# Down projection of three row blocks as seven block products, with the block sums made on GpSimd

## The chip, the cores and the metric

One core of one Trainium2 chip runs the whole program. The metric is the device time of one execution in microseconds (us), as the median of several runs. The engines are called PE (matrix products), DVE (vector), ACT (activations), POOL (GpSimd) and SP (which issues transfers).

## What is computed

The reference is one step of a one-layer trunk: an mLSTM and a gated MLP side by side, an output projection, and then a SwiGLU channel mixer. It runs over 2048 prompt rows and 8 sample rows, all in float32. The part that is changed is the last product, `@ w_down`:

```
h2 = rmsnorm(x, g_norm2) * (1 + sc2) + sh2
a, bb = jnp.split(h2 @ w_gate_up, 2, axis=-1)     # (T, 1024) @ (1024, 5632)
x = x + gt2 * ((jax.nn.silu(a) * bb) @ w_down)    # (T, 2816) @ (2816, 1024)
...
y = rmsnorm(x, g_final)
```

## The kernel before

The 2048 prompt rows go through in four blocks of 512 rows (`BLK`, `NBLK`). Every block passes the same stages: 24 slabs of `w_in` with the mixers in between, 8 slabs of `w_out`, the norm, 44 slabs of `w_gate_up`, and 22 slabs of `w_down`. Block 0 also carries the preparation of the modulation. The last block also carries the samples, and its down projection is not touched by the change.

Each float32 operand is split into a high part of reduced precision (`fp32r`) and the rest: `hi = round(x)`, `lo = x - hi`. A product is then three matmuls, hi by lo, lo by hi and hi by hi. A weight slab of 128x1024 elements lands in one of two slots of `raw` (a transfer that SP issues), ACT writes `w_hi` from it (`split_hi`), DVE writes `w_lo = raw - w_hi` (`split_lo`), and PE then uses both. The split of a slab may begin when PE is through with the slab two places earlier, and `raw` is loaded again when the slot's low part is done.

In the down stage a slab holds two k-tiles of 128 rows and half of the 1024 columns. PE runs over the block's four row tiles with it (`tile_product`), so a slab is 4 x 2 x 3 = 24 matmuls of 128x128 by 128x512. The first eleven slabs make the left 512 columns, the other eleven the right. After each half DVE takes the four PSUM banks, multiplies by the gate `gt2` and adds to `x1` (`down_tiles`). The activations, `act_hi` and `act_lo`, come from the gate-up stage, where `gate_tile` on DVE multiplies the two halves, ACT makes the high part and DVE the low part.

Beside this, the down stage prepares the next block: POOL loads the next 512 rows into `x_sb` and computes a root (`root`), ACT squares and scales, DVE scales (`scale_left`), PE transposes eight tiles (`norm_out`), ACT and DVE write `hT_hi` and `hT_lo` from them (`next_tiles`, `norm_tiles`). The order on each engine is written out by hand; engines wait for each other by semaphores, and every queue is worked off in order.

Of the kernel before, what the change touches and what calls it, by code (L numbers as in the profile page):

```python
# [29 lines left out]
P = 128  # L30
# [33 lines left out]
NSLAB = S_DOWN + N_DOWN  # L64
NORM_AT = (5, 7)
# [42 lines left out]
def hybrid_step(nc, x_prompt, x_sample, c_prompt, c_sample, state_C, state_n, state_m, w_ada, b_ada,  # L108
# [4 lines left out]
    with ctx:  # L113
# [29 lines left out]
        w_lo, WL = new("w_lo", [P, 2, KT, P], F32R)  # L143

# [15 lines left out]
        hm = place("hm", [P, TT, H, P], F32, U + 16 * kb)  # L160

# [116 lines left out]
        proj_rows = nc.dram_tensor("proj_rows", [NB, N_IN], F32).ap()  # L278

# [20 lines left out]
        DOWN_BANK = [T[0], T[1], G[0], G[1]]  # L300

# [20 lines left out]
        tile_ps = signal("tile_ps", 4 * (TT - 1))  # L322
        out_read = signal("out_read", 4 * TT, 1)
# [61 lines left out]

        def each_head(ap, n=P):

            return ap.unsqueeze(2).broadcast_to([ap.shape[0], ap.shape[1], n])
# [38 lines left out]
        def _(sp):  # L427
# [12 lines left out]
            def load_in(blk, s):  # L440
                c = IN_COLS[s % NSLAB]
                load(blk, s, in_v[:, :, c:c + P], KT)

# [12 lines left out]
            def sample_loads(s):  # L456
# [12 lines left out]
                if s == 6:  # L469
                    sp.wait_ge(sem("vo_ps"), 1)  # L470
# [27 lines left out]
            def sp_block(blk):  # L498
# [15 lines left out]
                for n in range(N_DOWN):  # L514
                    j, q = divmod(n, DOWN_Q)
                    load_pair(blk, S_DOWN + n, down_v, q, j)
                    if n == DOWN_Q + 4:
                        sp.wait_ge(out_read.sem, out_read.at(blk, 3 * TT))
                        gate_row(gt2_in, work[:, 1], 1, BLK, D)
                for s in (NSLAB, NSLAB + 1):  # L520
                    load_in(blk, s)
# [45 lines left out]
        def _(pool):  # L567
# [67 lines left out]
            def samples_state():  # L635
                pool.wait_ge(sem("wexp"), 2)
# [5 lines left out]
            def samples_mixing():  # L642
                done = sem("hcm")
                pool.wait_ge(sem("vars"), 1)
# [15 lines left out]
            def pool_block(blk, last):  # L660
# [4 lines left out]
                for c in range(TT):  # L665
# [11 lines left out]
                    if last and c == 0:  # L677
                        pool.wait_ge(sem("msml"), 1)
# [17 lines left out]
                if not last:  # L696
                    pool.wait_ge(zadd.sem, zadd.at(blk, 2 * TT))
# [36 lines left out]
            with pool.Fori(0, NBLK - 1) as blk:  # L734
                pool_block(blk, False)
# [4 lines left out]
        def _(act):  # L740
# [62 lines left out]
            def for_samples(step):  # L803

                if step == "SG":
                    act.wait_ge(sem("proj_in"), 48)
                    act.activation(proj[:, GATE0:], proj[:, GATE0:], ACT.Gelu_apprx_tanh)\
                        .then_inc(sem("gelus"), 1)
                    act.wait_ge(sem("nAs"), 1)
                    act.activation(sm["e"][:, :], sm["nA"][:, :], ACT.Exp).then_inc(sem("logs"), 1)  # L810
                    act.wait_ge(sem("logs"), 1)
                    act.activation(sm["l"][:, :], sm["e"][:, :], ACT.Ln, bias=1.0).then_inc(sem("logs"), 1)
                elif step == "SW":
                    act.wait_ge(sem("wargs"), 1)
                    act.activation(sm["quant"][:, 4:12], sm["quant"][:, 4:12], ACT.Exp)\
                        .then_inc(sem("wexp"), 1)
                    act.activation(sm["em"][:, :], sm["m"][:, :], ACT.Exp, scale=-1.0)\
                        .then_inc(sem("wexp"), 1)
                    fetch("small_out", m_sample[0], sm["m"][:, :])
                elif step == "SC":  # L820
                    act.wait_ge(sem("oTs"), 1)
                    act.activation(colq[:, 10], colq[:, 1], ACT.Sigmoid).then_inc(sem("sigs"), 1)
# [27 lines left out]
            def scale_right(blk):  # L850

                act.wait_ge(rs.sem, rs.at(blk, MEANS[1]))
                for i in range(TT):
# [4 lines left out]
            def norm_tile(blk, n, k, a_col, b_col):  # L858
# [4 lines left out]
                act.activation(work[:, 2 + k % 2], ps[:, :], ACT.Identity,  # L863
# [48 lines left out]
            def act_block(blk, last, first=False):  # L912
# [54 lines left out]
                def gate_pairs(pair_i):  # L967
                    for u in range(2):
# [3 lines left out]
                        if last and u == 1:  # L972
# [4 lines left out]
                        act.activation(act_hi[:, bass.ds(pair_i * 2 + u, 1), :], work[:, 3:4, :], ACT.Copy)\  # L977
                            .then_inc(act_hi_done.sem, 1)
# [25 lines left out]
                for n in range(N_DOWN):  # L1004
# [1258 lines left out]
```

## Time and profile before

| what | us |
|---|---|
| median of three runs (2477.85 to 2480.75) | 2479.61 |
| span of the profiled execution, first to last instruction | 2477.8 |
| PE busy in it | 2427.0 |
| DVE, ACT, POOL busy in it | 1203.8, 846.1, 176.9 |
| down stage of block 1, from 1121.56 to 1244.83 | 123.27 |
| of this DVE busy, ACT busy, POOL busy | 46.06, 36.48, 1.03 |

The page gives the profiled execution by its span alone; no time around it is listed for it. The median of the runs is 1.8 us above that span, the lowest run equal to it to 0.1 us. A matmul's row shows 0.39 us, but matmuls overlap in the pipeline: their cost is the distance from one start to the next. "Idle before" in a group is the time in which the engine stood still just ahead of that instruction, with what ended it.

### The profile page before, as it was taken

How to read it: one execution, taken by the hardware profiler on the slowest of the kernel's cores; microseconds unless marked ns; L12 is line 12 of the kernel's file. 1: busy time of each engine (PE TensorE's matmuls, PEld its weight loads, DVE VectorE, ACT ScalarE, POOL GpSimd, SP SyncE). 2: the span in 40 equal slices, each digit the busy share in tenths (PEclk: the TensorE clock that was granted, in tenths of full speed). 3: DMA queues.
4: the chain of work that ended last, by engine and by line, in shares of the span. 5: the costliest groups of instructions: out<-in, count | busy, mean ns of one | idle time of the engine just before them, and what ended most of it. 6: DMA issues, size and time to landing. Idle time of an engine off the chain costs nothing.

```text
span 2477.8 us, 32788 instructions
## 1 busy us (share of the span) xinstructions
PE 2427.0 (98%) x12296; PEld 1979.9 (80%) x12296; DVE 1203.8 (49%) x1773; ACT 846.1 (34%) x1152; POOL 176.9 (7%) x143
## 2 busy tenths in 40 slices
PE   5999999999999999999999999999999999999998
PEld 4688877888888878888888878888888878888776
DVE  4648544434346554444354754443449754333323
ACT  2333422233244243334143343333236323333212
POOL 0022000000003000000002200000002400000001
PEclk8999999999999999999999999999999999999999
DMA  7822365332352333332342233333255322222222
GB/s 280 287 80 90 111 196 164 118 95 96 91 147 66 101 111 99 96 93 94 103 140 78 90 111 98 97 93 102 94 185 160 92 77 69 85 85 85 89 90 86
DMA packets 361045, 280.14 MB, mean 113 GB/s; under 512 B 11289, under 2 KB 302653, under 8 KB 360920
## 3 DMA queue, kind: packets, MB, share of 16 engines
q1 hardware_dynamic: 333012, 228.91, 30.5%
q10 hardware_dynamic: 23956, 34.81, 4.1%
q0 software_dynamic: 3968, 14.95, 1.6%
q8 instruction: 71, 1.16, 0.2%
q14 instruction: 38, 0.30, 0.0%
HBM read 267.68 MB, written 10.96 MB: 112 GB/s over the span
## 4 chain that ended last, share of the span: by engine, by line
PE 89%; DVE 5%; issue 2%; DMA 2%; ACT 1%; POOL 0%; DVEq 0%; SPq 0%; ACTq 0%; POOLq 0%
PE banks L1862 18%; PE banks L1863 18%; PE banks L1864 18%; PE banks L1915 9%; PE banks L1916 8%; PE banks L1917 8%; PE banks L1742 1%; DVE w_lo L1337 1%; DMA stage<-in_w_ada_dram 1%; PE banks L1876 1%; PE banks L2004 1%; PE banks L2061 1%; PE banks L1886 1%; PE banks L1938 1%; PE banks L2030 1%
## 5 line engine op out<-in xcount | busy, mean ns | idle before, releaser
L1862 PE MATMUL banks<-hT_hi,w_lo 128*128 128x512 f32 x2176 | 859.9, 395 | 3.1 <-DVE hT_lo L1343 1.6
L1864 PE MATMUL banks<-hT_hi,w_hi 128*128 128x512 f32 x2176 | 848.6, 390 | 0.0
L1863 PE MATMUL banks<-hT_lo,w_hi 128*128 128x512 f32 x2176 | 848.5, 390 | 0.0
L1337 DVE TENSOR_TENSOR w_lo<-raw,w_hi 128x1024 fp32r<-128x1024 f32 x392 | 493.3, 1258 | 579.5 <-ACT w_hi L848 567.7
L848 ACT ACTIVATE w_hi<-raw 128x1024 fp32r<-128x1024 f32 x392 | 412.7, 1053 | 465.7 <-PE banks L1917 437.4
L1862 PEld LDWEIGHTS banks<-hT_hi,w_lo 128*128 128x128 f32 x2176 | 409.3, 188 | 100.6 <-issue 9.3
L1864 PEld LDWEIGHTS banks<-hT_hi,w_hi 128*128 128x128 f32 x2176 | 409.0, 188 | 86.2
L1863 PEld LDWEIGHTS banks<-hT_lo,w_hi 128*128 128x128 f32 x2176 | 409.4, 188 | 81.3
L1915 PE MATMUL banks<-w_lo,act_hi 128*128 128x512 f32 x704 | 276.2, 392 | 0.0
L1916 PE MATMUL banks<-w_hi,act_lo 128*128 128x512 f32 x704 | 274.2, 390 | 0.0
L1917 PE MATMUL banks<-w_hi,act_hi 128*128 128x512 f32 x704 | 274.1, 389 | 0.0
L1675 DVE TENSOR_TENSOR work<-work,banks 128x512 f32<-128x512 f32 x88 | 60.5, 688 | 271.9 <-ACT work L971 271.9
L977 ACT ACTIVATE act_hi<-work 128x512 f32 (+1 forms) x88 | 55.6, 632 | 371.8 <-DVE work L1679 371.8
L1915 PEld LDWEIGHTS banks<-w_lo,act_hi 128*128 128x128 f32 x704 | 132.1, 188 | 32.0 <-issue 4.5
L1917 PEld LDWEIGHTS banks<-w_hi,act_hi 128*128 128x128 f32 x704 | 132.1, 188 | 27.8
L1916 PEld LDWEIGHTS banks<-w_hi,act_lo 128*128 128x128 f32 x704 | 132.2, 188 | 26.7
L1679 DVE TENSOR_TENSOR work<-work,banks 128x512 f32<-128x512 f32 x88 | 60.6, 689 | 190.1 <-PE banks L1864 190.1
L587 POOL TENSOR_TENSOR rrt<-msq,half 128x1 f32<-128x1 f32 (+1 forms) x27 | 18.2, 676 | 1424.2 <-DVE msq L1098 1168.2
L971 ACT ACTIVATE work<-banks 128x512 f32<-128x512 f32 x88 | 52.6, 598 | 187.3 <-PE banks L1864 186.9
L1915 PE MATMUL banks<-w_lo,mix_hi 128*128 128x512 f32 x256 | 100.4, 392 | 1.8 <-DVE w_lo L1337 1.1
L1916 PE MATMUL banks<-w_hi,mix_lo 128*128 128x512 f32 x256 | 99.8, 390 | 0.0
L1917 PE MATMUL banks<-w_hi,mix_hi 128*128 128x512 f32 x256 | 99.6, 389 | 0.0
(335 smaller groups left out, 1828.9 us busy)
## 6 DMA issues: line engine op xcount, KB each, us to landing
raw<-in_w_gate_up_dram SPq DMA_DIRECT2D x176, 512.0 KB, 3.6
raw<-in_w_in_dram SPq DMA_DIRECT2D x96, 512.0 KB, 3.7
raw<-in_w_down_dram SPq DMA_DIRECT2D x88, 512.0 KB, 3.6
ada_stage<-in_w_ada_dram ACTq DMA_DIRECT2D x8, 2048.0 KB
raw<-in_w_out_dram SPq DMA_DIRECT2D x32, 512.0 KB, 3.6
in_stage<-in_w_in_dram ACTq DMA_DIRECT2D x6, 2048.0 KB
stage<-in_w_ada_dram SPq DMA_DIRECT2D x4, 2048.0 KB
x_sb<-in_x_prompt_dram POOLq DMA_DIRECT2D x4, 2048.0 KB, 8.8
```

The costliest lines, as they stand in the source:

```text
L848: act.activation(w_hi[:, s % 2], raw[:, s % 2], ACT.Copy).then_inc(hi_done.sem, 1)
L971: act.activation(work[:, 2], G[0][:, :], ACT.Sigmoid).then_inc(evac.sem, 1)
L977: act.activation(act_hi[:, bass.ds(pair_i * 2 + u, 1), :], work[:, 3:4, :], ACT.Copy)\
L1337: ve.tensor_tensor(w_lo[:, s % 2], raw[:, s % 2], w_hi[:, s % 2].bitcast(F32), ALU.subtract).then_inc(lo_done.sem, 1)
L1675: ve.tensor_tensor(work[:, 2], work[:, 2], G[0][:, :], ALU.mult).then_inc(silu_done.sem, 1)
L1679: ve.tensor_tensor(work[:, 3], work[:, 2], G[1][:, :], ALU.mult).then_inc(gated.sem, 1)
L1862: mm(out, w_lo[:, slot, k, :], rhs_hi[:, r, :], start=start and n == 0, stop=False)
L1863: mm(out, w_hi[:, slot, k, :], rhs_lo[:, r, :], start=False, stop=False)
L1864: ins = mm(out, w_hi[:, slot, k, :], rhs_hi[:, r, :], start=False, stop=stop and last)
L1915: mm(out, x_hi[:, k0 + k, t], lo[:, k, :], start=start and k == 0, stop=False)
L1916: mm(out, x_lo[:, k0 + k, t], hi[:, k, :], start=False, stop=False)
L1917: ins = mm(out, x_hi[:, k0 + k, t], hi[:, k, :], start=False, stop=stop and k == 1)
```

## The change

In blocks 0 to 2 the product A @ B of the down stage is cut in two by two: A by row halves (256 rows each) and by even and odd k-tiles, B by even and odd k-tiles and by column halves. Instead of the eight block products there are seven (the form of Strassen's scheme with 15 sums), named in the order in which they run: P1, P2, P5, P6, P7, P3, P4. Each has 11 k-tiles, two row tiles and 512 columns, so 66 matmuls of the same shape as before.

- **Weights.** The four sums of blocks of B are computed once, in block 0, by POOL (`down_sums`): 11 rounds of a 1 MB load, four subtractions of 128x512 and a 1 MB store to `wd_scratch` in DRAM. SP waits for all of them (`wd_out`) before it loads the first slab of P5 in each block. A product has six slabs of 2, 2, 2, 2, 1 and 2 k-tiles, 42 per block where there were 22, and they rotate through three slots: the two old ones and a third (`raw2` with `w2` or `w3`). The split of a slab may begin when PE is through with the slab three places earlier.
- **Activations.** `gate_tile` writes the float32 products into `quad`. High and low parts are made there for the row half that P1 and P2 use. POOL makes the four sums of blocks of A (`quad_sums`, `total`), each in pieces of 4, 4 and 3 k-tiles by 256 columns. For P5, P6, P7, P3 and P4 ACT makes the high parts (`high_part`) and POOL the low parts (`low_parts`), in the same pieces.
- **Results.** ACT copies P1 out of PSUM while P2 goes on accumulating on it. DVE joins the other products (`rows_11`, `sums_u`, `rows_with`), between its splits.
- **Next block.** The load of `x_sb` stands behind the sums on POOL, and its steps (squares, root, scaling, transposes) move to later slabs.
- **Names.** A number of one-time semaphores are merged (`STEPS`, `once`); that changes no instruction's work.

```diff
+SEVEN_K = ((0, 2), (2, 4), (4, 6), (6, 8), (8, 9), (9, QM))
+NSEV = 7 * len(SEVEN_K)
+PIECES = ((0, 4), (4, 8), (8, QM))
+P1, P2, P5, P6, P7, P3, P4 = range(7)
+NORM_AFTER = {31: (0, 1), 33: (2, 3), 37: (4, 5), 39: (6, 7)}
+SQUARES_AT = (20, 21, 22, 23)
+MEAN_AT, LEFT_AT, RIGHT_AT = 25, 28, (28, 29)
...
+            def down_sums():
+                pool.wait_ge(zadd.sem, zadd.at(0, 2 * TT))
...
+                for m in range(QM):
...
+                    pool.dma_start(wd_in[:, :, :], pairs_v[m]).then_inc(sem("wd_in"), 16)
+                    pool.wait_ge(sem("wd_in"), 16 * (m + 1))
...
+                    pool.tensor_tensor(wd_sums[:, 0], b12, b11, ALU.subtract).then_inc(done, 1)
...
+                    pool.dma_start(wd_scratch[:, :, m, :].rearrange("q p n -> p q n"), wd_sums[:, :, :])\
...
+            def quad_sums(blk):
+                def total(first, out, a, b, op):
+                    for i, (m0, m1) in enumerate(PIECES):
+                        pool.tensor_tensor(out(m0, m1), a(m0, m1), b(m0, m1), op).then_inc(quad_sum.sem, 1)
...
+                def low_parts(prod):
+                    for i, (m0, m1) in enumerate(PIECES):
+                        pool.wait_ge(part_hi.sem, part_hi.at(blk, n))
...
+                        pool.tensor_tensor(lo, piece_source(prod, m0, m1), hi.bitcast(F32), ALU.subtract)\
+                            .then_inc(part_lo.sem, 1)
+                pool.wait_ge(gated.sem, gated.at(blk, FT))
+                pool.wait_ge(act_ready.sem, act_ready.at(blk, FT))
+                total(0, s, a21, a22, ALU.add)
+                total(3, a21, a11, a21, ALU.subtract)
+                low_parts(P5)
+                total(6, s, s, a11, ALU.subtract)
+                low_parts(P6)
+                total(9, a12, a12, s, ALU.subtract)
...
                 if not last:
-                    pool.wait_ge(zadd.sem, zadd.at(blk, 2 * TT))
+                    if first:
+                        down_sums()
+                    low_parts = quad_sums(blk)
                     pool.dma_start(x_sb[:, :, :], x_v[bass.ds(blk + 1, 1)].rearrange("o p i d -> p (o i) d"))\
                         .then_inc(x_in.sem, 16)
                     pool.wait_ge(x_in.sem, x_in.at(blk, 32))
                     pool.sem_inc(x_next.sem, 1)
+                    low_parts(P7)
+                    low_parts(P3)
                     root(blk, 1)
+                    low_parts(P4)
...
+            def split_hi_seven(blk, n):
...
+                act.wait_ge(done.sem, done.at(blk, count))
+                act.wait_ge(slab_used.sem, slab_used.at(blk, S_DOWN + max(n - 2, 0)))
...
+                act.activation(sev_flat(dst, m1 - m0), sev_flat(src, m1 - m0), ACT.Copy).then_inc(hi_done.sem, 1)
...
+            def split_lo_seven(blk, n):
...
+                ve.wait_ge(hi_done.sem, hi_done.at(blk, S_DOWN + n + 1))
...
+                ve.tensor_tensor(lo, src, hi.bitcast(F32), ALU.subtract).then_inc(lo_done.sem, 1)
...
+            def gained(blk, i, row, j, gate, src):
+                link(ve.tensor_tensor(both(work[:, 0]), src, gate, ALU.mult))
+                out = x1[:, row, j * BLK:(j + 1) * BLK]
+                ve.tensor_tensor(out, out, work[:, 0], ALU.add).then_inc(zadd.sem, 1)
...
+            def rows_with(blk, prod, j, gate, parts, row0, count):
+                for i in range(2):
+                    product_ready(blk, prod, i)
+                    link(ve.tensor_tensor(both(work[:, 0]), parts[i], both(SEVEN_BANK[prod][i]), ALU.add))
...
+                    gained(blk, 2 * TT + count + i + 1, row0 + i, j, gate, both(work[:, 0]))
...
-                for n in range(1, N_DOWN + 1):
-                    if n < N_DOWN or not last:
-                        split_lo(blk, S_DOWN + n)
...
+                split_lo(blk, S_DOWN + 1)
+                for n in range(NSEV + 1):
+                    seven_out(blk, n)
+                    if n + 2 < NSEV:
+                        split_lo_seven(blk, n + 2)
...
+            def seven_products(blk):
+                for n in range(NSEV):
...
+                    pe.wait_ge(lo_done.sem, lo_done.at(blk, S_DOWN + n + 1))
+                    for i in range(2):
...
+                        for m in range(m0, m1):
...
+                            if i == 0 and prod > P2 and m % 4 == 0:
+                                pe.wait_ge(part_lo.sem, part_lo.at(blk, 3 * (prod - P5) + m // 4 + 1))
...
+                            mm(out, x_hi, low, start=start, stop=False, skip_group_check=True)
+                            mm(out, x_lo, high, start=False, stop=False, skip_group_check=True)
+                            ins = mm(out, x_hi, high, start=False, stop=stop, skip_group_check=True)
...
+                    ins.then_inc(slab_used.sem, 1)
+                    if n in NORM_AFTER:
...
+                        norm_out(blk, NORM_AFTER[n])
```

On POOL, in the loop over blocks, these rows stood between the last root of the norm (`rrt<-msq,half 128x1`) and the root for the next block (`128x4`); ISA and REGISTER_ALU rows are waits:

```order
L587 TENSOR_TENSOR rrt<-msq,half 128x1
L697 ISA
L698 ISA
L698 DMA x_sb<-in_x_prompt_dram 128x4x1024
L700 REGISTER_ALU
L595 REGISTER_ALU
L587 TENSOR_TENSOR rrt<-msq,half 128x4
```

At the same place POOL now begins with these; `s_quad` and `quad` are sums of activation blocks, `part` the high and low parts, and a size of 128x4x256 is 1024 elements per partition:

```order
L808 ISA
L809 REGISTER_ALU
L793 TENSOR_TENSOR s_quad<-quad 128x1024 x2
L793 TENSOR_TENSOR s_quad<-quad 128x768
L794 ISA
L793 TENSOR_TENSOR quad<-quad 128x4x256 x2
L793 TENSOR_TENSOR quad<-quad 128x3x256
L794 REGISTER_ALU
L802 ISA
L804 TENSOR_TENSOR part<-s_quad,part 128x4x256
```

Until the row that loads `x_sb` there are 18 of these operations in all, and 9 more follow it; before there was none.

On DVE, at the end of the left half of the down stage, the four tiles of results followed on a split (two of the four are shown; `x_56` is `x1`):

```order
L1337 TENSOR_TENSOR w_lo<-raw,w_hi 128x1024
L1506 ISA
L1482 REGISTER_ALU
L1514 TENSOR_TENSOR work<-banks,work 128x512
L1074 REGISTER_ALU
L1516 TENSOR_TENSOR x_56<-x_56,work 128x512
```

Now DVE comes to its first results, those of P2, after the split of slab 13, and the next row is the split of slab 14:

```order
L1747 TENSOR_TENSOR w_lo<-raw,w_hi 128x1024
L1766 ISA
L1752 ISA
L1769 TENSOR_TENSOR work<-banks,work 128x512
L1286 REGISTER_ALU
L1772 TENSOR_TENSOR x_56<-x_56,work 128x512
L1769 TENSOR_TENSOR work<-banks,work 128x512
L1286 REGISTER_ALU
L1772 TENSOR_TENSOR x_56<-x_56,work 128x512
L1745 REGISTER_ALU
L1747 TENSOR_TENSOR w_lo<-raw_61,w_hi 128x1024
```

So each group of results stands in front of the split of the slab that PE uses two slabs later.

## Rows read from the trace of the kernel before

**Rows 1.** Page, head and part 1: busy time, share of span, instructions of each engine.
```profile
span 2477.8 us, 32788 instructions
PE 2427.0 (98%) x12296; PEld 1979.9 (80%) x12296; DVE 1203.8 (49%) x1773; ACT 846.1 (34%) x1152; POOL 176.9 (7%) x143
```

**Rows 2.** Windows, gate-up stage of block 0 and down stage of block 1; columns in line 1.
```profile
core 0: us, PE busy (x) PEld busy (x) DVE busy (x) ACT busy (x) POOL busy (x), PEclk, DMA share, GB/s
284.00:542.00 258.00, 257.68 (x1214) 204.49 (x1213) 124.18 (x154) 75.58 (x96) 0.85 (x1) 1.00 0.47 148
1121.70:1244.70 123.00, 123.00 (x561) 102.23 (x560) 46.06 (x57) 36.48 (x43) 1.03 (x1) 1.00 0.30 97
```

**Rows 3.** Timeline of PE, down stage of block 1, first matmuls and last: start us, us, what.
```profile
1121.56 0.39 PE L1915 MATMUL banks<-w_lo,act_hi 128*128 128x512 f32 x1
1121.78 0.39 PE L1916 MATMUL banks<-w_hi,act_lo 128*128 128x512 f32 x1
...
1244.60 0.39 PE L1917 MATMUL banks<-w_hi,act_hi 128*128 128x512 f32 x1
1244.83 0.39 PE L1984 MATMUL banks<-hT_lo,gw 128*128 128x512 f32 x1
```

**Rows 4.** Chain of waits, one of block 1's two rows of transposes: start, us, what.
```profile
1154.37 1.75 PE banks L1961 x16
```

**Rows 5.** Groups by line and form: count, busy us, mean ns, idle before.
```profile
L848 ACT ACTIVATE w_hi<-raw 128x1024 fp32r<-128x1024 f32 x392 | 412.7, 1053 | 465.7 <-PE banks L1917 437.4 <-DMA raw<-in_w_in_dram 16.8 <-DMA raw<-in_w_down_dram 9.1
L1337 DVE TENSOR_TENSOR w_lo<-raw,w_hi 128x1024 fp32r<-128x1024 f32 x392 | 493.3, 1258 | 579.5 <-ACT w_hi L848 567.7 <-issue 0.9 <-DVE proj_gates L1156 0.3
L1516 DVE TENSOR_TENSOR x<-x,work 128x512 f32<-128x512 f32 x32 | 22.2, 693 | 4.8 <-DVE work L1514 3.5
L1342 DVE CAST hT_hi<-work 128x512 fp32r<-128x512 f32 x64 | 27.0, 422 | 28.6 <-ACT work L863 28.3
L706 POOL TENSOR_TENSOR x<-x,g_fin 128x512 f32<-128x512 f32 x4 | 5.0, 1283 | 122.6 <-ACT junk L766 122.6
L689 POOL TENSOR_TENSOR vs_tm<-vs_tm,rln 128x2048 f32<-128x2048 f32 x4 | 14.4, 3612 | 0.7 <-DVE vs_tm L1449 0.7
```

**Rows 6.** Timelines of POOL and DVE in block 0: two collisions, one operation alone.
```profile
206.21 3.61 POOL L689 TENSOR_TENSOR vs_tm<-vs_tm,rln 128x2048 f32<-128x2048 f32 x1 [0.16 <-DVE vs_tm L1449]
206.74 4.17 DVE L1337 TENSOR_TENSOR w_lo<-raw,w_hi 128x1024 fp32r<-128x1024 f32 x1 [0.64 <-ACT w_hi L848]
...
177.70 2.09 POOL L629 TENSOR_TENSOR hm<-hm,rml 128x512 f32<-128x512 f32 x1
177.66 1.22 DVE L1337 TENSOR_TENSOR w_lo<-raw,w_hi 128x1024 fp32r<-128x1024 f32 x1 [1.14 <-ACT w_hi L848]
...
218.73 1.04 POOL L629 TENSOR_TENSOR hm<-hm,rml 128x512 f32<-128x512 f32 x1
```

**Rows 7.** Timelines of POOL and DVE in block 0: overlap without a delay.
```profile
157.36 1.29 POOL L621 TENSOR_TENSOR decay<-decay,mask 128x512 f32<-128x512 f32 x1
157.14 0.69 DVE L1420 TENSOR_TENSOR work<-banks,col 128x516 f32<-128x516 f32 x1
```

**Rows 8.** Timeline of PE behind the first collision of rows 6.
```profile
212.81 0.39 PE L1864 MATMUL banks<-hT_hi,w_hi 128*128 128x512 f32 x1
213.77 0.46 PE L2061 MATMUL banks<-wT,vs_tm 128*128 128x128 f32 x2 [0.57 <-DVEq L1422]
```

**Rows 9.** Windows at the program's start; PEclk is the third column from the end.
```profile
28.00:34.00 6.00, 0.90 (x7) 0.00 (x0) 3.56 (x7) 1.06 (x1) 1.04 (x1) 0.50 1.02 347
34.00:38.00 4.00, 3.90 (x20) 3.62 (x24) 1.51 (x4) 0.00 (x0) 0.64 (x1) 0.50 0.56 153
38.00:40.00 2.00, 2.00 (x18) 0.44 (x11) 0.09 (x1) 0.00 (x0) 0.00 (x0) 0.97 0.39 115
```

**Rows 10.** Page, part 6, DMA issues: KB each, us from issue to landing.
```profile
raw<-in_w_down_dram SPq DMA_DIRECT2D x88, 512.0 KB, 3.6
x_sb<-in_x_prompt_dram POOLq DMA_DIRECT2D x4, 2048.0 KB, 8.8
```

More of the change, by code:

```diff
@@ L661, in pool_block @@
+            def pool_block(blk, last, first=False):
                 if last:
@@ L732, in sample_root @@
                 power(sem("s_root"), s_r[:, :], s_ms[:, :], NB, P)
-            with pool.Fori(0, NBLK - 1) as blk:
+            pool_block(0, False, first=True)
+            with pool.Fori(1, NBLK - 1) as blk:
                 pool_block(blk, False)
@@ new lines, in sums_u @@
+            def sums_u(blk):
+                for i in range(2):
+                    product_ready(blk, P6, i)
+                    ve.wait_ge(u_set.sem, u_set.at(blk, i + 1))
+                    ve.tensor_tensor(work[:, 2 + i], work[:, 2 + i], SEVEN_BANK[P6][i], ALU.add).then_inc(sev_read.sem, 1)
+                for i in range(2):
+                    ve.wait_ge(sev_read.sem, sev_read.at(blk, 3 + i))
+                    ve.tensor_tensor(t_sum[i], both(work[:, 2 + i]), both(SEVEN_BANK[P5][i]), ALU.add)\
+                        .then_inc(sev_read.sem, 1)
@@ L1690, in ve_block @@
                     thin_in_rows(TH_IN + N_TH_IN - 1)
-                with ve.Fori(2 * N_TH_IN if first else 0, FT) as i:
-                    gate_tile(i)
+                if last:
+                    with ve.Fori(0, FT) as i:
+                        gate_tile(i)
+                else:
+                    with ve.Fori(N_TH_IN if first else 0, QM) as m:
+                        for kappa in range(2):
+                            gate_tile(m * 2 + kappa, m, kappa)
                 ve.wait_ge(slab_used.sem, slab_used.at(blk, S_DOWN))
@@ L2189, in pe_block @@
                     pe.transpose(N2[0:H, 0:P], CN[:, :, P], ident[:, :]).then_inc(sem("fin_ps"), 1)
-                for n in range(N_DOWN):
+                if not last:
+                    seven_products(blk)
+                for n in range(N_DOWN if last else 0):
                     j, q = divmod(n, DOWN_Q)
@@ L2221, in pe_block @@
                         samples()
-                    if n in NORM_AT and not last:
-                        c = 4 * NORM_AT.index(n)
-                        norm_out(blk, range(c, c + 4))
             pe_block(0, False, first=True)
```

372 lines of the change are left out of this document (288 added, 84 removed).

## The prediction

> **What bounds the kernel now.** I read the page's busy shares first: PE is busy for 2427.0 of 2477.8 us, no other engine for half of that [rows 1]. [...] The stage runs from 1121.56 to 1244.83, that is 123.27 us [rows 3]. Two transpose rows of 1.75 us lie in it [rows 4], so its 528 matmuls take 119.77 us and one costs 0.2268 us. That is the price of a matmul here; the 0.39 us in its row is the length in the pipeline. So fewer matmuls pay in full, as long as the other engines keep the splits ahead. In this stage a split by ACT takes 1.05 us and one by DVE 1.22 [rows 5, 6], and a slab gives PE 24 x 0.2268 = 5.44 us of work.
>
> **The change part by part.**
>
> Matmuls. Seven products of 66 are 462 instead of 528 per block. 66 x 0.2268 = 14.97 us go per block, and PE's own work in the stage becomes 123.27 - 14.97 = 108.3 us. Over three blocks that is 44.9 us, 1.8%. The transposes stay.
>
> Slabs. Each is now half as long for PE, 12 x 0.2268 = 2.72 us (the sixth one-k-tile slab of a product, 1.36), while its split costs the same, for ACT 1.05 and for DVE 1.22. By the third slot a split may start two slabs, 5.44 us, before PE needs it. 1.05 + 1.22 = 2.3 us fit, with 3.1 to spare. At the start there is less: slab 1 waits for the last gate-up slab, then a DVE product (0.69, as the row of L1516 [rows 5]), a high part of 256 columns (between a quarter and a half of the 1.05 us for 1024, say 0.4) and both splits, 3.4 us against 2.72, so 0.7 us are lost. The loads land 3.6 us after issue [rows 10] and start when the slab three places earlier is split, so I cost them at nothing; their cover is those same 5.44 us and more.
>
> POOL's sums. Per block 27 operations, 18 of 1024 elements per partition and 9 of 768. POOL needs 1.283 us for 512 elements from two different operands [rows 5]. With one operand broadcast it needs 1.04 for 512 and 3.612 for 2048 [rows 5, 6], so 1.674 ns per element and 0.18 us fixed. With that fixed part the first price gives 2.15 ns per element: 2.39 us for 1024, 1.83 for 768, in all 9 x (2 x 2.39 + 1.83) = 59.5 us. The lower bound is the broadcast rate, 1.90 and 1.47, in all 47.4 us; 1.283 us for each 512, with nothing saved by length, would be 63.5 us at the top. I take 59.5, since L706 reads two full operands as these sums do. [...]
>
> What these sums do to DVE. The trace shows that POOL and DVE do not work side by side when both read two operands from SBUF. At 206.21 POOL began an operation of 3.61 us; DVE's split issued at 206.74 ended at 210.91, after 4.17 us instead of 1.22 [rows 6]. The other way round, at 177.66 a split of 1.22 us was running, and POOL's 1.04 us became 2.09 [rows 6]. A DVE operation with one operand in PSUM was not held up: 0.69 us under POOL's 1.29 [rows 7]. So I count the time of such operations on both engines as one resource. Whole operations alternate, not their elements.
>
> The sum of that resource, from the end of gate-up until P4 begins (36 slabs; the low parts for P4 are due there too). POOL: 59.5. DVE: 31 full splits at 1.22 are 37.8, six half ones at 0.69 are 4.2, six operations on results with both operands in SBUF at 0.69 are 4.2, a low part 0.35, four scalings at 0.42 and four tiles of the next block at 0.42 + 0.69 are 6.1; in all 52.6 (the 0.69 and 0.42 from L1516 and L1342 [rows 5]). Together 112.1 us. PE has 396 x 0.2268 + 1.75 = 91.6 us of work in the same stretch. So the bound moves from PE to what POOL and DVE share, by 20.5 us. P4 with its transposes adds 66 x 0.2268 + 1.75 = 16.7 us, undisturbed: 128.8. The shared resource also stands idle once: POOL waits 8.8 us for the load of `x_sb` [rows 10], while DVE can split only as fast as PE frees slots, 8.8 / 2.72 x 1.22 = 3.9 us. That leaves 4.9 us idle, and the low parts for P7 and P3 queue behind the wait. The stage becomes 133.7 us, 10.4 longer than before: 15.0 us of matmuls saved, 25.4 us of waits gained.
>
> Where they fall: at slabs 1 and 2, where POOL's six sums start as gate-up ends; at each short slab of P1 and P5, where 1.36 us of matmuls cover a pair of 2.39 + 1.22; and, largest, some 6 us each at slabs 14 and 32, where DVE has two to four result operations in front of the split and POOL gets a turn before each.
>
> The weights' sums. 44 operations of 128x512 in block 0, 44 x 1.28 = 56 us, in a stage of 258 us where DVE is busy for 124 [rows 2]. A split there has 3.1 us to spare and meets one operation of 1.28, seldom two. I take 1 us; bounds 0 and 5 (0.5 us for ten slabs). Their transfers, 22 of 1 MB, go beside slabs that land with 7 us to spare.
>
> Block ends. The results of P4 reach `x1` some 4 us after the last matmul, under the 16 gate matmuls (3.6 us) with which PE begins the next block; I cost that at nothing, 0.5 us a block if the cover fails.
>
> Sum: 3 x 10.4 + 1 = 32 us. The profiled span is 2477.8 and the median 2479.6; I add to the median: 2511.6, rounded to 2511.
>
> **The rivals.**
>
> A, faster: the collisions are absorbed. After the 4.17 us split PE had matmuls until 212.81 and stood still for only 0.57 us, on another wait [rows 8]. If POOL and DVE meet as rarely as that, the stage takes 108.3 plus the 0.7 at its start and up to 3.5 us behind the result groups, 109 to 112.5 us, and the time is 2480 - 3 x 11 to 14, some 2444. It decides from the point where collisions cost PE less than 15.0 of the 25.4 us per block counted above. Against it: there the slab was 5.44 us long and the collision single.
>
> B, no change: POOL works at the broadcast rate. 47.4 in place of 59.5 leaves 3 x 1.7 us less than before by the sum, or a little over it where turns do not mesh: 2474 to 2486, say 2480. For it, that L706 is only 512 elements long; against, that the operand that repeats is what makes the other rows cheap.
>
> C, slower still. Waits of 6 us can bring the clock down. [...] Two such waits per block are 12 us in all. And 2 MB for `x_sb` now land beside twice the weight traffic; 3 us later is 9 us over three blocks. Together 2532. [...]
>
> D, the weight sums are not there in time for P5 of block 0. They have 258 us for 11 rounds, 23 us each; a round is 5.1 us of sums, and two transfers of 1 MB, by half of 8.8 each, 14 us in all. I give it no chance of its own.
>
> **How the numbers follow.** The forecast, 2490 to 2525, has 0.53; C 0.12; B 0.14; A 0.21. Faster than 0.2% (below 2474.6, about what a measurement of this kernel can tell) is A: 0.21. Within 0.2% is most of B: 0.10. Slower is the rest: 0.69. The range reaches into A and takes in B and most of C, 2466 to 2536.
>
> **What would show it.** In the profile of the changed kernel: matmul distance still 0.227 us; down stages of 130 to 137 us in blocks 0 to 2 with some 25 us of PE idle, ended by `w_lo`, most at slabs 1, 5, 14, 17 and 32; POOL's pieces at 2.4 us or more each; the mean of the DVE split in these stages near 2.5 us in place of 1.26; PE without waits in the last block. Right in mechanism but wrong in size would be splits that are held up while PE idles under 10 us per stage. Wrong altogether would be splits near 1.3 us beside POOL's sums.

## The result, and the profile after

The changed kernel takes 2532.41 us (median of 4 runs, 2531.02 to 2533.86), the kernel before beside it 2479.34 (2477.85 to 2480.75): a ratio of 1.0215, 95% interval 1.0201 to 1.0230. It is 53 us slower; the prediction said 32 slower, with 2466 to 2536 as its range.

The page of the changed kernel, head and part 1, answers to [rows 1]:

```profile
span 2532.2 us, 33213 instructions
PE 2414.6 (95%) x12098; PEld 1955.0 (77%) x12098; DVE 1398.1 (55%) x1863; ACT 925.6 (37%) x1263; POOL 487.1 (19%) x290
```

PE has 198 matmuls fewer, as was meant (3 x 66). Yet it is busy for only 12.4 us less, and the span grew by 54.4. DVE is busy for 194 us more and POOL for 310.

The down stage of block 1 in windows that are cut at PE's three long waits; it answers to the second row of [rows 2], and the columns are the same:

```profile
1147.50:1151.00 3.50, 0.46 (x3) 0.05 (x1) 3.33 (x2) 2.03 (x3) 3.50 (x2) 1.00 0.00 0
1151.00:1157.00 6.00, 6.00 (x19) 4.75 (x20) 6.00 (x3) 0.63 (x1) 5.92 (x3) 0.72 0.43 121
...
1187.50:1193.20 5.70, 0.36 (x2) 0.00 (x0) 5.42 (x4) 1.36 (x2) 5.70 (x3) 0.94 0.00 0
1193.20:1199.20 6.00, 5.97 (x14) 4.72 (x15) 5.42 (x2) 0.45 (x1) 5.92 (x3) 0.50 0.65 192
...
1245.50:1252.20 6.70, 0.33 (x3) 0.09 (x2) 6.54 (x4) 2.55 (x4) 5.50 (x3) 0.87 0.00 0
1252.20:1258.20 6.00, 5.99 (x16) 4.76 (x17) 3.67 (x6) 0.58 (x1) 0.00 (x0) 0.57 0.74 248
```

In the windows of 3.5, 5.7 and 6.7 us PE does next to nothing, while DVE is busy nearly all the time and POOL for most of it. In the 6 us behind each PE is busy throughout, at a granted clock of 0.72, 0.50 and 0.57 (at 0.50 a matmul starts every 0.43 us, in place of every 0.227). That costs (1 - clock) x 6 us: 1.7 + 3.0 + 2.6 = 7.3 us.

PE's timeline: the stage's first matmul, the ends of these waits, and the row behind the stage; it answers to [rows 3]:

```profile
1145.03 0.39 PE L2245 MATMUL banks<-w_lo,part 128*128 128x512 f32 x1
...
1150.95 0.49 PE L2245 MATMUL banks<-w_lo,part 128*128 128x512 f32 x1 [3.04 <-DVE w_lo L1549]
...
1193.23 0.79 PE L2245 MATMUL banks<-w_lo,part 128*128 128x512 f32 x1 [5.37 <-DVE w_lo L1747]
...
1252.21 0.79 PE L2245 MATMUL banks<-w_lo,part 128*128 128x512 f32 x1 [6.38 <-DVE w_lo L1747]
...
1282.80 0.39 PE L2320 MATMUL banks<-hT_lo,gw 128*128 128x512 f32 x1
```

All three are waits for a slab's low part from DVE, at slabs 1, 14 and 32. The last row is the first matmul of the next block, so the stage ends at 1282.80, after 137.77 us; those of blocks 0 and 2 took 134.69 and 137.07.

DVE's groups by form in this stage (count, busy us, mean ns, idle before), which answer to the splits in [rows 5]:

```profile
L1747 DVE TENSOR_TENSOR w_lo<-raw,w_hi 128x1024 fp32r<-128x1024 f32 x33 | 65.0, 1994 | 19.3 <-ACT w_hi L1022 18.5 <-DVE x L1760 0.5
L1747 DVE TENSOR_TENSOR w_lo<-raw,w_hi 128x512 fp32r<-128x512 f32 x7 | 11.3, 1608 | 2.6 <-ACT w_hi L1022 2.6
```

What stood at 1.22 and 0.69 us takes 1.99 and 1.61 here. The instructions are the same; the rest is waiting that the profile counts as their own time. POOL's row for the stage shows the other side, 77.96 us busy where the sum had 59.5 plus a root.

So the 54.4 us of the span are: the down stages +11.4, +14.5 and +13.8 us (39.7 together), the gate-up stage of block 0 +11.9 (the first down stage starts at 554.21, before it was 542.27), 0.9 between the down stages, and some 2 us behind the last one.

### The profile page after: what moved, and what is told of

Read it like the earlier page. It is cut to its first block, busy times and chain, and to the rows that moved or that the text cites. A ratio compares the mean times of both kernels' runs of the same rounds, so it can differ in the third digit from the quotient of the medians.

```text
span 2532.2 us, 33213 instructions
## 1 busy us (share of the span) xinstructions
PE 2414.6 (95%) x12098; PEld 1955.0 (77%) x12098; DVE 1398.1 (55%) x1863; ACT 925.6 (37%) x1263; POOL 487.1 (19%) x290
## 3 DMA queue, kind: packets, MB, share of 16 engines
q8 instruction: 70, 1.15, 0.2%
## 4 chain that ended last, share of the span: by engine, by line
PE 72%; DVE 11%; DMA 5%; POOL 5%; issue 4%; ACT 2%; DVEq 0%; SPq 0%; ACTq 0%; POOLq 0%
PE banks L2165 17%; PE banks L2166 17%; PE banks L2167 17%; PE banks L2218 4%; PE banks L2219 4%; PE banks L2220 4%; DVE w_lo L1747 3%; DMA raw<-in_w_gate_up_dram 2%; DVE w_lo L1549 2%; POOL s_quad L793 1%; POOL quad L793 1%; POOL part L804 1%; PE banks L2045 1%; PE banks L2245 1%; DMA stage<-in_w_ada_dram 1%
## 5 line engine op out<-in xcount | busy, mean ns | idle before, releaser
L1549 DVE TENSOR_TENSOR w_lo<-raw,w_hi 128x1024 fp32r<-128x1024 f32 x332 | 430.1, 1296 | 416.5 <-ACT w_hi L1012 407.1
L1012 ACT ACTIVATE w_hi<-raw 128x1024 fp32r<-128x1024 f32 x326 | 342.8, 1051 | 250.5 <-PE banks L2220 208.4
L1747 DVE TENSOR_TENSOR w_lo<-raw,w_hi 128x1024 fp32r<-128x1024 f32 (+1 forms) x120 | 228.1, 1931 | 62.0 <-ACT w_hi L1022 60.1
L2245 PE MATMUL banks<-w_lo,part 128*128 128x512 f32 x462 | 192.8, 417 | 55.6 <-DVE w_lo L1747 46.2
L1957 DVE TENSOR_TENSOR work<-work,banks 128x512 f32<-128x512 f32 x88 | 60.5, 688 | 272.0 <-ACT work L1171 272.0
L2246 PE MATMUL banks<-w_hi,part 128*128 128x512 f32 x462 | 187.1, 405 | 0.0
L2247 PE MATMUL banks<-w_hi,part 128*128 128x512 f32 x462 | 186.7, 404 | 0.0
L1022 ACT ACTIVATE w_hi<-raw 128x1024 fp32r<-128x1024 f32 (+1 forms) x120 | 117.6, 983 | 186.9 <-PE banks L2247 122.6
L2245 PEld LDWEIGHTS banks<-w_lo,part 128*128 128x128 f32 x462 | 91.4, 198 | 88.5 <-issue 40.9
L793 POOL TENSOR_TENSOR s_quad<-quad 128x1024 f32<-128x1024 f32 (+1 forms) x9 | 25.4, 2843 | 588.9 <-DVE part L1965 588.9
L1963 DVE TENSOR_TENSOR quad<-work,banks 128x512 f32 (+1 forms) x66 | 45.4, 688 | 152.7 <-PE banks L2167 152.7
L2247 PEld LDWEIGHTS banks<-w_hi,part 128*128 128x128 f32 x462 | 90.9, 197 | 20.5
L2246 PEld LDWEIGHTS banks<-w_hi,part 128*128 128x128 f32 x462 | 91.5, 198 | 18.1
```

Source lines behind the costliest of these rows:

```text
L1012: act.activation(w_hi[:, s % 2], raw[:, s % 2], ACT.Copy).then_inc(hi_done.sem, 1)
L1022: act.activation(sev_flat(dst, m1 - m0), sev_flat(src, m1 - m0), ACT.Copy).then_inc(hi_done.sem, 1)
L1549: ve.tensor_tensor(w_lo[:, s % 2], raw[:, s % 2], w_hi[:, s % 2].bitcast(F32), ALU.subtract).then_inc(lo_done.sem, 1)
L1747: ve.tensor_tensor(lo, src, hi.bitcast(F32), ALU.subtract).then_inc(lo_done.sem, 1)
L2245: mm(out, x_hi, low, start=start, stop=False, skip_group_check=True)
L2246: mm(out, x_lo, high, start=False, stop=False, skip_group_check=True)
```

## The experiments

Two places were to be explained: the down stages, and block 0's gate-up stage. The table has all runs. "Start" is the first matmul of block 0's down stage; stages are from there to the next block's first gate matmul; "between" runs from the end of one down stage to the start of the next, over blocks 1 and 2. All in us. Stages are read from the profiled execution, the time is the median; E8's profiled execution took 2449.9, 4 less than its median. E1, E2, E3, E6, E7 and E9 are one run each, E4, E5 and E8 eight, eleven and five.

| kernel | start | down stages | between | time |
|---|---|---|---|---|
| before | 542.3 | 123.3, 123.3, 123.3 | 456.0, 456.1 | 2479 |
| changed | 554.2 | 134.7, 137.8, 137.1 | 456.1, 456.9 | 2532 |
| E1 small sums | 548.6 | 111.8, 113.7, 112.3 | 456.1, 456.9 | 2454 |
| E2 powers of 4 columns | 558.7 | 113.2, 114.3, 114.1 | 456.1, 456.9 | 2471 |
| E9 powers of 10 columns | 554.4 | 115.1, 115.2, 114.2 | 456.1, 457.1 | 2469 |
| E3 low parts on DVE | 551.2 | 128.7, 128.9, 129.3 | 456.1, 457.2 | 2506 |
| E7 split first | 548.7 | 133.4, 137.0, 136.7 | 456.2, 456.7 | 2524 |
| E6 first round later | 546.5 | 135.2, 138.4, 136.6 | 456.1, 457.8 | 2528 |
| E4 early, paced | 549.2 | 119.6, 121.2, 121.1 | 458.9, 459.7 | 2485 |
| E5 spread | 549.4 | 117.0, 116.0, 116.6 | 461.9, 463.2 | 2477 |
| E8 aligned | 543.1 | 112.3, 113.4, 112.6 | 456.1, 457.4 | 2454 |

### Is it what POOL does, or the new order of the slabs?

E1 cuts POOL's 27 sums per block to 8 columns (where so cut, P5 and P6 take their activations from `quad`):

```diff
-pool.tensor_tensor(out(m0, m1), a(m0, m1), b(m0, m1), op).then_inc(quad_sum.sem, 1)
+pool.tensor_tensor(out(m0, m1)[:, :, 0:8], a(m0, m1)[:, :, 0:8], b(m0, m1)[:, :, 0:8], op)...
```

> Left out: in the down stages of blocks 0 to 2 POOL's 27 sums are made for 8 of 256 columns only, so what P5, P6, P7, P3 and P4 multiply is not the reference's; the weights' sums in block 0 stay whole. Theory (POOL's and DVE's operations on two SBUF operands take turns): with POOL's operations this short, the turns are gone. The down stages of blocks 1 and 2, 137.8 and 137.1 us, become 109 to 114 (108.3 of PE's own work and 1 to 6 of starts and result groups), PE's gaps of 3.0, 5.3 and 5.8 us at slabs 1, 14 and 32 shrink below 1.5, and the granted clock in them is 1.00 again. Gate-up of block 0 stays 12 us longer than before. Time 2532 - 23 - 2 x 25 = 2459, between 2450 and 2468. Rival 1 (the half-length slabs and their order are at fault, not the sums): stages stay above 130, time above 2510. Rival 2 (the clock falls for another reason than the waits): gaps go, but the mean clock of the stages stays at 0.95.

Measured: 2454.0 us. In block 1 the gap at slab 1 is 1.15 us, at slab 14 there is none, at slab 32 it is 0.6; the largest of all is 1.4, at slab 20. The stage as one window, in columns as in [rows 2], and DVE's full splits in it:

```profile
1116.45:1230.10 113.65, 109.47 (x496) 89.75 (x494) 71.39 (x86) 68.23 (x81) 12.85 (x29) 1.00 0.62 194
...
L1748 DVE TENSOR_TENSOR w_lo<-raw,w_hi 128x1024 fp32r<-128x1024 f32 x33 | 40.2, 1227 | 34.1 <-ACT w_hi L1023 33.1 <-DVE x L1761 0.5
```

The mean granted clock is 1.00 over the stage, and the splits take 1.23 us again. The 42 short slabs and the longer chain of results cost 3.5 to 5.4 us beside PE's 108.3, no more (111.8 to 113.7). Rivals 1 and 2 fall, and the matmuls saved do pay in full.

E2 and E9 keep POOL at work but let it touch little. A power of a few columns is slow on POOL for its size, 1.14 to 1.17 us for the 4 columns of E2 and 2.01 to 2.10 for the 10 of E9 (E9's edit):

```diff
-pool.tensor_tensor(lo, piece_source(prod, m0, m1), hi.bitcast(F32), ALU.subtract)
+pool.tensor_tensor(lo[:, 0, 0:10], onerow[:, 0:10], half[:, 0:10], ALU.pow)
```

> Left out: POOL's 27 sums per block are replaced by a power of 4 columns of constants, some 2.5 us each, so POOL is about as long at work but touches little; and in block 0, 40 of the 44 subtractions of weights are made for 8 columns only, while their transfers stay whole. Theory (turns): in the trace of before a POOL power of 3.8 us did not hold a DVE split up, so the down stages become 109 to 118 us although POOL is as busy as in the changed kernel, and DVE's splits return to 1.2 to 1.4 us. Rival (POOL is simply late with sums and low parts): stages stay above 130. Gate-up of block 0: if its 12 us come from the transfers, it stays 8 to 12 us longer than before; if from the subtractions, 0 to 3 us. Time by theory and transfers 2450 to 2475; by the rival above 2510.

> Left out: as in E2, POOL's 27 sums per block are replaced by powers of constants and 40 of the 44 subtractions of weights in block 0 are made for 8 columns; the transfers stay whole. Two edits on E2: the powers are made of 10 columns, since those of 4 took only 1.1 us and POOL was not as busy as in the changed kernel; and the first round waits for the first gated tile as in E6. Priced between 1.10 us for 4 columns and 3.81 for 16, 10 columns take 2.4 us, 27 of them 66 us. Theory (turns on operations with two SBUF operands): DVE's splits stay at 1.22 and 0.69 us, POOL's lateness alone costs little: stages 111 to 118 us at a clock of 1.00. Rival (POOL's sums and low parts are late, whatever they touch): 130 to 138 us. Block 0: with its subtractions all but gone, what its down stage starts later than 542.3 is the transfers' alone: theory 3 to 9 us, 545 to 551; rival (subtractions are the cause) below 544. Time 2452 to 2472 by theory, above 2510 by the rival.

(The power of 3.8 us that the expectation of E2 names began at 202.25, behind a split that ran from 202.08; it could not have held that split up. E9 fills this gap.)

Measured: 2471.4 and 2469.1 us. E2's powers were mispriced (1.1 us each, not 2.5), so its stages of 113 to 114 us say no more than E1's. E9 is the one that decides. Its groups on POOL and DVE in the down stage of block 1 (POOL's three over the whole stage, then DVE's over 1125 to 1210):

```profile
L805 POOL TENSOR_TENSOR part<-onerow,half 128x10 fp32r<-128x10 f32 x15 | 31.3, 2096 | 27.8 <-ACT part L1046 17.7 <-DMA x_sb<-in_x_prompt_dram 10.1
L794 POOL TENSOR_TENSOR s_quad<-onerow,half 128x10 f32<-128x10 f32 x6 | 12.5, 2101 | 248.2 <-DVE part L1965 248.1
L794 POOL TENSOR_TENSOR quad<-onerow,half 128x10 f32<-128x10 f32 x6 | 11.9, 2006 | 0.2
...
L1747 DVE TENSOR_TENSOR w_lo<-raw,w_hi 128x1024 fp32r<-128x1024 f32 x25 | 30.4, 1224 | 26.9 <-ACT w_hi L1022 26.4
L1747 DVE TENSOR_TENSOR w_lo<-raw,w_hi 128x512 fp32r<-128x512 f32 x5 | 3.5, 693 | 9.0 <-ACT w_hi L1022 9.0
```

POOL is busy with the 27 for 31.3 + 12.5 + 11.9 = 55.7 us, near the 59.5 of the sum, in the same places of the order, and it still waits 10.1 us for `x_sb`. DVE's splits are back at 1.22 and 0.69 us, and the stage takes 115.2. Over the whole stage 25 of the 42 splits began while a power was running, and none took more than 1.23 us; in the changed kernel 25 of 42 overlap one of POOL's operations and take up to 3.43, the other 17 at most 1.23. So it is neither POOL's lateness nor its order that stretches the splits, but POOL's sums themselves, which read and write 768 or 1024 elements per partition: such a sum and a DVE operation on two SBUF operands take turns. A power of 10 columns does not keep DVE from its work, though it too has two SBUF operands; whether that is the operation or its few columns, no run here tells.

### Is it the sum that counts, or the order at two places?

E7 lets DVE make the split two slabs ahead before it takes a product's results; E3 moves the 15 low parts from POOL (2.4 us for 1024 elements) to DVE (1.2). E7's edit:

```diff
 for n in range(NSEV + 1):
+    if n + 2 < NSEV:
+        split_lo_seven(blk, n + 2)
     seven_out(blk, n)
-    if n + 2 < NSEV:
-        split_lo_seven(blk, n + 2)
...
```

> Everything is computed. One edit on the changed kernel: DVE makes the split two slabs ahead before the result group of a product (not after the last one). Theory 1 (the sum of POOL's and DVE's operations sets the stage): the sum is the same, so the gaps of 5.4 and 5.8 to 6.4 us at slabs 14 and 32 shrink, but others grow as much or nearly: stages 132 to 137 us, time 2520 to 2532. Theory 2 (it is the order at these two places, with room elsewhere): both gaps fall below 2.5 us, nothing else grows and the clock stays up: stages 124 to 130, time 2495 to 2514.

> Everything is computed; the 15 low parts per block move from POOL to DVE, at 1.22 us for 1024 and 0.95 for 768 in place of 2.39 and 1.83. Theory (one shared resource): before P4, 12 of them count, 8 x 1.17 + 4 x 0.88 = 12.9 us less on the resource, and three low parts for P7 and three for P3 no longer queue behind the wait for x_sb: stages 122 to 130 us in place of 137, time 2532 - 3 x 7 to 14 = 2490 to 2511, some 2503. Rival (DVE is the bound by itself, as it does the splits): the stages get longer, by up to 14 us of operations moved to it, time above 2532.

Measured for E7: 2524.1 us, stages 133.4 to 137.0. In block 1 the gap of 5.4 at slab 14 is now one of 5.2 at slab 15; that of 6.4 at slab 32 is one of 3.3 at slab 33, with a new one of 2.0 at slab 27. The sum did not change, and nor did the stage by more than 1.3 us: theory 1. (5.5 of the 8 us by which its time is shorter lie in block 0's gate-up, which E7 doesn't touch.)

Measured for E3: 2506.4 us, stages of 128.7 to 129.3, 6 to 9 less, of the 7 to 14 that the sum gave. The gap at slab 14 fell to 1.4, but one of 7.2 appeared at slab 23: POOL waits for DVE's low parts before its last three sums, so `x_sb` is loaded late, ACT stands for 9.37 us at the squares of `x_sb`, and the splits stand behind them on ACT's queue. The rival, that DVE is the bound by itself, falls; the later load had not been priced.

### Block 0's gate-up stage

E6 lets the first of the eleven rounds of weights' sums wait for the first gated tile:

```diff
-pool.wait_ge(zadd.sem, zadd.at(0, 2 * TT))
+pool.wait_ge(gated.sem, gated.at(0, 1))
```

> Everything is computed. One edit on the changed kernel: the first round of the weights' sums in block 0 waits for the first gated tile of gate-up, 5 to 10 us later than now. Theory: that round met DVE's split of the second norm's tiles, on which PE waits there; PE's gaps of 2.1 and 1.2 us at 294 to 297 and the 3 us that the clock of 0.84 costs until 310 go, and the down stage of block 0 starts at 545 to 549 in place of 554.2; what stays above 542.3 is late slabs beside the 22 transfers. Time 2532 - 6 = 2526. Rival (only the transfers count): no change, the stage starts at 551 to 555, time 2530 to 2534. The start at 548.6 and 551.2 in E1 and E3, whose block 0 was the same up to there, says that the transfers' share differs from run to run by some us.

Measured: 2527.7 us, start 546.5, 7.7 less. The stage's first 16 us in the changed kernel, in columns as in [rows 2]:

```profile
284.00:300.00 16.00, 12.71 (x67) 10.12 (x66) 14.44 (x18) 8.35 (x10) 7.63 (x7) 0.84 0.52 174
```

And in E6:

```profile
284.00:300.00 16.00, 15.67 (x89) 12.71 (x88) 12.27 (x20) 9.91 (x12) 0.00 (x0) 1.00 0.27 77
```

In the first row POOL's subtractions meet DVE's low parts of the second norm (`hT_lo`), for which PE waits there: it is busy for 3.0 us less than in E6, and the clock of 0.84 costs another 2.6. So the collision is worth some 5.5 us of the 11.9, and E6 gives it back; the rest of E6's gain is within what the transfers differ by from run to run (below).

What stays of E6's start, 4.2 us over before, is mostly transfers. E2 and E9 had all transfers and almost no subtractions, so their rounds followed each other faster, and their starts are the latest of all, 558.7 and 554.4; E2's, 16.4 us over before, holds the first round's collision too, but E9's, with none there, is 12.1 us of transfers. Both are more than was expected, 12 and 9 at most. The rival that only subtractions count falls. The DMA issues of the stretch 300 to 460 (KB each, median us to landing), before:

```profile
raw<-in_w_gate_up_dram SPq DMA_DIRECT2D x26, 512.0 KB, 3.6
in_stage<-in_w_in_dram ACTq DMA_DIRECT2D x6, 2048.0 KB
```

The same in the changed kernel:

```profile
raw<-in_w_gate_up_dram SPq DMA_DIRECT2D x26, 512.0 KB, 6.7
wd_scratch<-wd_sums POOLq DMA_DIRECT2D x9, 1024.0 KB, 6.0
wd_in<-in_w_down_dram POOLq DMA_DIRECT2D x9, 1024.0 KB, 9.0
```

Six transfers of 2 MB for block 0's own preparation already ran there. With 18 of 1 MB beside them a slab lands after 6.7 us instead of 3.6 (7.5 in E9, where 22 fall into this stretch), and PE waits up to 2.2 us for one. In three of the four longest of these waits the late slab's split met a subtraction as well and took 1.4 to 1.7 us instead of 1.2. The share of this part differs from run to run: E1 and E3 had the same code up to the start of the down stage as the changed kernel, and started 5.6 and 3.0 us sooner. E8 (below), which moves the first round and spreads the others, starts 0.8 us after before: both parts can be avoided.

### A version that keeps the gain

If the turns are the cause, the remedy is to take POOL's operations out of the stage in which DVE is needed. E4 makes the low parts on DVE, the twelve sums on POOL during gate-up as the tiles of a piece are ready, the split first as in E7, and spreads the rounds of block 0:

```diff
+for i, (m0, m1) in enumerate(PIECES):
+    pool.wait_ge(gated.sem, gated.at(blk, 2 * m1))
...
+    for step, (out, a, b, op) in enumerate(((s, a21, a22, ALU.add), (a21, a11, a21, ALU.subtract),
+                                            (a11, s, a11, ALU.subtract), (a12, a12, a11, ALU.subtract))):
+        pool.tensor_tensor(out[:, m0:m1], a[:, m0:m1], b[:, m0:m1], op).then_inc(quad_sum.sem, 1)
...
```

> Everything is computed. Four edits: low parts on DVE; POOL makes the twelve sums piece by piece during gate-up; DVE makes the split two slabs ahead before the result group of a product; the rounds of the weights' sums in block 0 are spread, one every 1.75 gated tiles (20.5 us). Theory: on the shared resource before P4 there are then only DVE's own 52.6 us and 12 low parts of 1.22 and 0.95, 13.6 us; 66 us against 91.6 of PE, so PE is the bound again. Stages of blocks 1 and 2 at 111 to 118 us, block 0 at 112 to 122; gate-up of block 0 back to 258 to 263 us; gate-up of blocks 1 and 2 up to 3 us longer by the early sums. Time 2532 - 2 x 22 - 18 - 9 + 4 = 2465, between 2445 and 2480. Rival 1 (collisions only move into gate-up): gate-up of blocks 1 and 2 longer by 10 us or more each, time above 2485. Rival 2 (the transfers themselves, however spread, cost the 12 us of block 0): gate-up of block 0 above 266.

Measured: 2485.43 us, ratio 1.0026 (1.0015 to 1.0037), 5 us above the range expected. The stages fell by 15 to 17 us, the larger part of what was expected, but not all: a gap of 2.5 at slab 1 (the last piece's sums), 2.4 beside the load of `x_sb`, which now stands earlier, and the clock after both (0.72 in the 6 us behind each, block 1). The early sums cost 2.8 us per gate-up stage, and block 0's first round was left where it was, so its start came only 5.0 us sooner. E5 takes on these places, with the early sums one per gated tile:

> Everything is computed. E4 with four edits at the places where its trace showed waits: the early sums come one per gated tile in place of four in a row, those of the last piece one at a time behind slabs 1, 5, 7 and 9 of the down stage; x_sb is loaded in four parts of 0.5 MB, one every two slabs; the first round of weights' sums in block 0 waits for the first gated tile. Theory: E4's gaps (2.5 us at slab 1 from the last piece's sums; 3.0 us some 40 us into the stage from slabs that landed late beside 2 MB of x_sb; the clock at 0.83 to 0.96 after each) go: stages 119.6, 121.2 and 121.1 become 111 to 115; gate-up of blocks 1 and 2 ends 1.5 to 2.8 us sooner; gate-up of block 0 ends 5 to 7 us sooner, at 542 to 545. Time 2485 - 3 x 8 - 2 x 2 - 6 = 2451, between 2442 and 2460. Rival (with POOL's sums spread they meet a DVE split more often, one delay each): gate-up of blocks 1 and 2 longer than 460 us from stage to stage, time above 2465.

Measured: 2477.26 us where 2451 was expected, ratio 0.9991 (0.9982 to 1.0000), no difference from before, since the rival held: with the sums spread one per gated tile, "between" rose to 461.9 and 463.2. POOL's and DVE's timelines of E5 show why:

```profile
984.18 2.40 POOL L807 TENSOR_TENSOR quad<-quad 128x1024 f32<-128x1024 f32 x1 [9.25 <-DVE part L1963]
984.35 3.31 DVE L1540 TENSOR_TENSOR w_lo<-raw,w_hi 128x1024 fp32r<-128x1024 f32 x1 [0.40 <-ACT w_hi L1003]
```

The signal that let POOL begin came 0.15 to 0.3 us ahead of a split, each of the eight times in this stage; the split took 3.2 to 3.3 us, and PE then stood still for 0.3 to 0.5. E8 lets the sum begin where DVE has just ended a split and has no work on two SBUF operands for the next 4 us; it also loads `x_sb` by rows, three slabs apart, the gate's right half four slabs later, and spreads block 0's rounds further:

```diff
 pool.wait_ge(gated.sem, gated.at(blk, tiles))
+pool.wait_ge(lo_done.sem, lo_done.at(blk, S_UP + 2 * tiles + 3))
...
+for i in range(TT - 1):
+    pool.wait_ge(part_lo.sem, part_lo.at(blk, i + 1))
+    pool.wait_ge(slab_used.sem, slab_used.at(blk, S_DOWN + 9 + 3 * i))
```

> Everything is computed. E5 with three edits. The early sums start when DVE has just ended the second split of a gated tile, not when it is about to begin the next: in E5 each began within 0.3 us of a split, which took 3.2 to 3.3 us in place of 1.2, and PE stood still for 0.45 us each time, eight times a block. x_sb is loaded by rows as s_quad is given up, one at slab 6 and the others three slabs apart, and the gate's right half four slabs later, since in E5 the slab at 48 us into the stage landed 3.9 us late and cost a gap of 1.8 to 2.6 us with the clock at 0.79 behind it. The rounds of the weights' sums wait for odd gated tiles, since E5's second round followed the first at once and cost 2.75 us at 330. Theory: from stage to stage 456 to 458 us in place of 461.9 and 463.2; stages 112 to 115 in place of 116 to 117; block 0's stage starts at 543 to 547 in place of 549.4. Time 2477 - 11 - 3 x 3 - 4 = 2453, between 2444 and 2463. Rival (turns are taken at random, alignment gains nothing): stage to stage stays above 460, time above 2468.

Measured: 2454.15 us, ratio 0.9903 (0.9889 to 0.9917): faster than both kernels, and 1 us from the number expected. POOL and DVE in its gate-up stage of block 1:

```profile
978.70 2.40 POOL L810 TENSOR_TENSOR quad<-quad 128x1024 f32<-128x1024 f32 x1 [7.14 <-DVE w_lo L1543]
977.31 1.23 DVE L1543 TENSOR_TENSOR w_lo<-raw,w_hi 128x1024 fp32r<-128x1024 f32 x1 [0.26 <-ACT w_hi L1006]
983.61 1.23 DVE L1543 TENSOR_TENSOR w_lo<-raw,w_hi 128x1024 fp32r<-128x1024 f32 x1 [0.37 <-ACT w_hi L1006]
```

The down stage of block 1 as one window, in columns as in [rows 2]:

```profile
1111.53:1224.88 113.35, 110.04 (x496) 89.41 (x495) 91.17 (x100) 68.51 (x81) 12.72 (x9) 1.00 0.63 193
```

Both splits take 1.23 us again, with the sum between them. DVE is busy for 91 of 113 us in the stage, twice what it was before, and that costs PE little: its gaps in this stage come to 3.3 us, where the changed kernel had 19.1.

## Why the prediction was right, and where its terms were not

The sign and the mechanism held; the size was 21 us short: 8.5 of them in the down stages, 10.9 in block 0's gate-up, the rest behind the last stage and between the others. That rival C named 2532, the measured time, is luck: its 12 us for the clock and 9 for the load hold nothing for block 0. Taken in the order of its steps:

**Matmuls, right.** E1 and E8 show stages of 112 to 114 us, of which 108.3 are the 462 matmuls and the transposes.

**Slabs, nearly.** The start was costed at 0.7 us; without collisions slab 1 costs a gap of 1.1 to 1.4 us (E1, E8), with them 3.04.

**POOL's sums, right.** 2.39 us were taken for 1024 elements and 1.83 for 768; where nothing stands in their way they take 2.40 (the row of E5 above) and 1.81 to 1.85 (E4, E5).

**Turns, right.** E9 shows without the arithmetic that it is the sums. Two groups of the changed kernel over 1145 to 1283 show it within one kernel:

```profile
L1760 DVE TENSOR_TENSOR x<-x,work 128x512 f32<-128x512 f32 x4 | 4.8, 1199 | 0.1
L1769 DVE TENSOR_TENSOR work<-banks,work 128x512 f32<-128x512 f32 x2 | 1.4, 684 | 0.0
```

The first has two SBUF operands and takes 1.20 us in the mean where it took 0.69 [rows 5]; the second, of the same length, has one operand in PSUM and is not held up, as in [rows 7]. The mean of the full splits was to be near 2.5 us and is 1.99 in block 1: 17 of the 42 splits met no sum.

**The sum of the shared resource, right to some 3%.** It gave 112.1 + 4.9 = 117.0 us until P4 begins, and 16.7 for P4. Measured are 117.5, 120.1 and 119.4 until P4's first matmul, and 17.2 to 17.7 after it. The stage was to take 133.7 and took 134.7, 137.8 and 137.1: 8.5 us more in all.

**The split of that into waits and work, not right.** 25.4 us of waits were forecast; in block 1 PE stands idle for 19.1, with 1.8 more in the lengths of the matmuls ahead of the eleven gaps (0.39 shown less 0.23 of distance). In its place PE's own work became 7.3 us longer by the clock. Rival C had named that and priced it at 2 us per wait, what PE lost from 34 to 38 in [rows 9] (4 us of work at a granted 0.50), for two waits; in block 1 there are three, at 1.7 to 3.0. If the end of the stretch is set by the sum of POOL and DVE, as forecast, a slower clock takes its time mostly out of PE's idle time; that fits, since 20.9 + 7.3 is only 2.8 over the 25.4. But it is argued, not shown: no run had the waits without the clock.

**The weights' sums, wrong: 1 us was taken, with 0 to 5 as bounds, and 11.9 were measured.** Two steps failed. The collision was priced against a split in the middle of gate-up, with 3.1 us to spare; the first round fell on the low parts of the second norm, on which PE waits at once, and with the clock that is 5.5 us (E6). And the transfers were laid beside slabs that "land with 7 us to spare", without the six loads of 2 MB that run in the same stretch; that, with a few stretched splits, is the other 6.4 in the profiled run, and 0.8 and 3.4 in E1 and E3 (they started 6.3 and 8.9 us after before, the 5.5 among them).

**Where the waits fall, right:** slabs 1, 14 and 32 have the long ones, as `w_lo` was to end them. At the short slab 5 it is 0.8 to 0.9 us and at slab 17 at most 0.4, less than named; at slab 2 it is under 0.3. **Block ends:** nothing was taken, and "between" is the same to 0.8 us; the cause of some 2 us behind the last stage stays open.

The rest of the range: rival A needed collisions that PE hardly feels, and fell with 17.5 to 19.2 us of PE idle per stage; rival B needed sums at the broadcast rate, 1.90 us, and fell with their 2.40. The loads of `x_sb` took 11.1 us from issue to landing in the median, 2.3 more than in [rows 10], where rival C had 3. Rival D, the weights' sums being late for P5, didn't come up: the last round ended at 464, and POOL then stood idle for 93 us.

## What to carry to other kernels

Before work is handed to POOL because it is idle, add up POOL's and DVE's operations that read two operands of some length from SBUF, stage by stage, as if they were one engine's: if that sum passes PE's time in the stage, the engine that looked free is the new bound. Here the sum was 112.1 us beside 91.6 of PE until P4 begins, and the stretch took 117.5 to 120.1. The same operations cost next to nothing in a stage that has room, if each begins where DVE has just finished and not where it is about to begin ("between" is 456.1 and 457.4 in E8, 461.9 and 463.2 in E5, 456.0 and 456.1 before). And a new transfer is to be priced against all the traffic of the very stretch where it lands, not against the stretch whose rows are at hand.

## What was not expected of the hardware

A power on POOL, 55.7 us of it in one stage, leaves DVE's operations at their undisturbed length (E9), where 59.5 us of sums stretch them from 1.22 to 1.99 us. A split that began 0.17 us behind a sum of 2.40 took 3.31 us, as if it had stood until the sum was done and then run its 1.22 (E5); beside the powers of 10 columns, which read SBUF too, the splits took 1.224 us in the mean and none more than 1.23 (E9). What a wait of PE costs behind it does not follow from its length alone. The granted clock of the 6 us behind was 0.72 after a wait of 3.0 us, 0.50 after 5.4 and 0.57 after 6.4 (changed kernel, block 1), but 0.74 after one of 7.2 (E3, block 1), 0.72 after 1.8 (E5, block 1) and 1.00 after 2.2 (E9, block 1).
